# A two-layer diffusion step: the zeroing, three weight places, one modulation unit and one semaphore are moved

## The reference

```
for i in (0, 1):
    sh_a, sc_a, g_a, sh_f, sc_f, g_f = split(silu(cond) @ w_ada[i] + b_ada[i], 6)   # one set for context, one for latent
    h = layernorm(x) * (1 + sc_a) + sh_a
    out = diff_attention(h) @ w_attn_out   if i == 0   else   fourier_mix(h) @ w_fourier_out
    x = layernorm(alpha * x + g_a * out) * ln_gain[i, 0] + ln_bias[i, 0]
    h = layernorm(x) * (1 + sc_f) + sh_f
    y = sum over the top 2 of 8 experts in the top 1 of 4 groups of  w * (silu(h @ w_gate) * (h @ w_up)) @ w_down
    x = layernorm(alpha * x + g_f * y) * ln_gain[i, 1] + ln_bias[i, 1]
```

## Time and profile before

| | |
|---|---|
| median of 3 runs | 1018.64 us (1015.99 to 1021.48) |
| the profiled execution's own time | 1015.99 us |
| its span | 1014.2 us |
| its granted TensorE clock, mean | 0.933 of full speed |
| TensorE matmul busy | 852.1 us (84%) |
| VectorE, ScalarE, GpSimd busy | 342.7, 147.6, 164.8 us |
| moved by DMA | 324.69 MB, mean 320 GB/s |

### The profile page before, as it was taken

The page is one execution under the profiler, slowest core; times in us unless marked ns, Lnnn a source line. Parts: engine busy times, 40 slices in busy tenths (PEclk is TensorE's granted clock), DMA queues, the critical chain, the costliest instruction groups (busy, mean ns, idle before and its releaser), DMA issues.

```text
span 1014.2 us, 12948 instructions
## 1 busy us (share of the span) xinstructions
PE 852.1 (84%) x4983; PEld 441.9 (44%) x4983; DVE 342.7 (34%) x836; ACT 147.6 (15%) x341; POOL 164.8 (16%) x250
## 2 busy tenths in 40 slices
PE   3899999998997889988788787999599878787864
PEld 2556565655475333333233335766433333332321
DVE  3113455565784111111111159347511111111147
ACT  1122222224011010110000113111111000100010
POOL 1041111122112020211111001211111111111100
PEclk9999999999987999999899999999589989998988
DMA  9996584267368996999999779863889999999941
GB/s 336 366 370 242 182 327 177 84 251 261 125 238 348 375 415 267 418 418 419 418 420 418 321 299 388 306 248 137 328 350 419 419 419 418 418 421 417 392 170 62
DMA packets 91181, 324.69 MB, mean 320 GB/s; under 512 B 12590, under 2 KB 25614, under 8 KB 66520
## 3 DMA queue, kind: packets, MB, share of 16 engines
q1 hardware_dynamic: 73360, 287.97, 72.0%
q0 software_dynamic: 12704, 21.86, 6.0%
q10 hardware_dynamic: 5032, 13.71, 3.4%
HBM read 313.75 MB, written 32.05 MB: 341 GB/s over the span
## 4 chain that ended last, share of the span: by engine, by line
PE 54%; DMA 29%; DVE 10%; issue 3%; ACT 2%; POOL 1%; SPq 1%; ACTq 0%; POOLq 0%; DVEq 0%
PE psum L993 17%; DMA ring<-in_w_expert_up 16%; PE psum L876 8%; PE psum L823 6%; PE psum L1015 5%; DMA h_hT<-in_w_expert_up 4%; PE psum L772 4%; PE psum L848 3%; DMA ring<-in_w_ada 3%; PE psum L980 2%; DMA arena<-h_scratch,gidx 2%; DMA y_scratch<-arena,sidx 1%; PE psum L1204 1%; PE psum L1078 1%; PE psum L927 1%
## 5 line engine op out<-in xcount | busy, mean ns | idle before, releaser
L993 PE MATMUL psum<-ring,arena 128*64 128x512 f32 x880 | 267.2, 648 | 39.0 <-DMA ring<-in_w_expert_up 25.6
L993 PEld LDWEIGHTS psum<-ring,arena 128*64 128x64 f32 x880 | 88.1, 149 | 175.5 <-issue 172.0
L1015 PE MATMUL psum<-ring,arena 128*64 128x512 f32 x440 | 125.8, 603 | 20.1 <-DVE arena L1781 19.4
L1777 DVE TENSOR_TENSOR arena<-arena,psum 128x256 f32<-128x256 f32 x34 | 14.3, 421 | 296.8 <-ACT arena L1328 296.8
L993 PE MATMUL psum<-h_hT,arena 128*64 128x512 f32 x208 | 101.9, 647 | 10.2 <-DMA ring<-in_w_expert_up 9.3
L876 PE MATMUL psum<-ring,h_hT 128*128 128x384 f32 x288 | 98.0, 494 | 0.0
L823 PE MATMUL psum<-ring,h_hT 128*128 128x512 f32 x160 | 69.5, 593 | 1.1 <-ACT h_hT L1412 0.7
L876 PEld LDWEIGHTS psum<-ring,h_hT 128*128 128x128 f32 x288 | 54.4, 194 | 34.9 <-issue 1.6
L636 POOL DMA_INDIRECT y_scratch<-arena,sidx x32 | 32.7, 1021 | 227.0 <-DVE arena L1787 227.0
L1015 PEld LDWEIGHTS psum<-ring,arena 128*64 128x64 f32 x440 | 36.0, 137 | 71.3 <-issue 46.9
L772 PE MATMUL psum<-ring,silu 128*32 128x128 f32 x1536 | 52.7, 299 | 14.5 <-DMA ring<-in_w_ada 14.5
(11 more groups left out here) (207 smaller groups left out, 914.1 us busy)
## 6 DMA issues: line engine op xcount, KB each, us to landing
ring<-in_w_expert_gate SPq DMA_DIRECT2D x52, 1024.0 KB, 17.2
ring<-in_w_expert_up SPq DMA_DIRECT2D x52, 1024.0 KB, 23.9
ring<-in_w_expert_down SPq DMA_DIRECT2D x52, 1024.0 KB, 25.8
ring<-in_w_ada SPq DMA_DIRECT2D x24, 2048.0 KB, 15.1
h_hT<-in_w_expert_gate SPq DMA_DIRECT2D x12, 1024.0 KB, 18.2
h_hT<-in_w_expert_up SPq DMA_DIRECT2D x12, 1024.0 KB, 22.8
h_hT<-in_w_expert_down SPq DMA_DIRECT2D x12, 1024.0 KB, 25.6
ring<-in_w_qkv SPq DMA_DIRECT2D x9, 1024.0 KB, 12.4
```

The source lines that it names most:

```text
L993: last = pe.matmul(bank[b][64 * e:64 * e + 64, :].rearrange("p (g n) -> p g n", g=2), mem.GT[b][:, c, 64 * e:64 * e + 64], w, start=(c == ...
L1015: last = pe.matmul(bank[5 + half][64 * e:64 * e + 64, :], mem.actT[b][:, f, 64 * e:64 * e + 64], w[:, f, 512 * half:512 * half + 512], sta ...
```

## The change

1. **Zeroing.** The two transfers that zero `y_scratch` (3 MB each, from SBUF to DRAM) stood in the attention, one behind each of the last two quarters of `w_qkv`. Both now stand behind expert 0 of layer 0, ahead of unit (1, 1).
2. **Places.** Units (1, 3), (1, 4), (1, 5) go from C1, A0, A1 to A0, A1, A2. C1 is so free after unit (1, 1), and expert 1 of layer 0 is loaded then, not after unit (1, 3). Unit (1, 3) is now loaded when `w_attn_out` has been used, with (1, 4), and unit (1, 5) when (1, 2) has been computed.
3. **Unit (1, 9)** is computed ahead of the Fourier product of the context, not ahead of (1, 8); its add on VectorE moves ahead of the evictions of the turned tiles. Its transfer stays where it was.
4. **Semaphores.** `lam_in` is dropped: all seven transfers count on `ctx_in`, and both VectorE (before the lambda products) and TensorE (before the attention) wait for 16 * 7. The transpose of the condition counts on a new `cond_ps`, and the waits on `col_ps` are one lower.

```diff
-PLACE.update({("ada", 1, u): place for u, place in enumerate(("A2", "C1", "A2", "C1", "A0", "A1"))})
+PLACE.update({("ada", 1, u): place for u, place in enumerate(("A2", "C1", "A2", "A0", "A1", "A2"))})
...
             for u in (2, 3):
                 sp.wait_ge(qkv_ps, 6 * u - 6)
                 load_qkv(u, slice(0, 8), place_in[f"Q{u % 2}"])
-                sp.wait_ge(zeroed, 5)
-                sp.dma_start(y_dram[u - 2].rearrange("(c p) n -> p c n", p=P), bc(mem.zero.unsqueeze(1), [P, 2 * TILES, D])
-                             ).then_inc(scratch_out, 16)
...
             load("ada", 1, 0)
             sp.wait_ge(qkv_ps, 18)
             load_expert(0, 0)
+            sp.wait_ge(zeroed, 5)
+            for l in range(2):
+                sp.dma_start(y_dram[l].rearrange("(c p) n -> p c n", p=P), bc(mem.zero.unsqueeze(1), [P, 2 * TILES, D])
+                             ).then_inc(scratch_out, 16)
             sp.wait_ge(qkv_ps, 24)
             load("ada", 1, 1)
-            for u in (2, 3):
-                after_ada(1, u - 2)
+            after_ada(1, 0)
+            load("ada", 1, 2)
+            after_ada(1, 1)
+            load_expert(0, 1)
+            sp.wait_ge(proj_ps, 6)
+            for u in (3, 4):
                 load("ada", 1, u)
-            sp.wait_ge(proj_ps, 6)
-            for u in (4, 5):
-                load("ada", 1, u)
-            after_ada(1, 3)
-            load_expert(0, 1)
+            after_ada(1, 2)
+            load("ada", 1, 5)
             after_ada(1, 5)
...
-            pe.wait_ge(ctx_in, 32)
+            pe.wait_ge(ctx_in, 16 * 7)
...
             over_channels(0)
             pe.wait_ge(sums_read, 2)
+            ada(1, 9)
             pe.wait_ge(chan_act, 4)
...
-            for u in (9, 8, 10, 11):
+            for u in (8, 10, 11):
                 ada(1, u)
...
-                act.dma_start(mem.lam[:, n, :], A[name][0].partition_broadcast(P)).then_inc(lam_in, 16)
-            act.dma_start(mem.gain8[:, :], A["subln_gain"][0].partition_broadcast(P)).then_inc(lam_in, 16)
+                act.dma_start(mem.lam[:, n, :], A[name][0].partition_broadcast(P)).then_inc(ctx_in, 16)
+            act.dma_start(mem.gain8[:, :], A["subln_gain"][0].partition_broadcast(P)).then_inc(ctx_in, 16)
             act.dma_start(mem.ctxk, A["cache_k"][0, 0].rearrange("s h d -> s (h d)")).then_inc(ctx_in, 16)
             act.dma_start(mem.ctxv, A["cache_v"][0, 0].rearrange("s h d -> s (h d)")).then_inc(ctx_in, 16)
...
-            dve.wait_ge(lam_in, 16 * 5)
+            dve.wait_ge(ctx_in, 16 * 7)
...
             layer_end()
+            ada_add(1, 9)
             dve.wait_ge(col_done, 3)
             turn_evict(1, 1)
             turn_evict(1, 2)
-            for u in (9, 8, 10, 11):
+            for u in (8, 10, 11):
                 ada_add(1, u)
```

More of the change, by code:

```diff
@@ L282, in build @@
         h_dram = [nc.dram_tensor(f"h_scratch{l}", (2 * TOK, D), F32).ap() for l in range(2)]
-        first_in, router_in, x_in, lam_in, ctx_in = (sem(n) for n in ("first_in", "router_in", "x_in", "lam_in", "ctx_in"))
+        first_in, router_in, x_in, ctx_in = (sem(n) for n in ("first_in", "router_in", "x_in", "ctx_in"))
         spread_in, root_out = sem("spread_in"), sem("root_out")
@@ L291, in build @@
         down_landed = [sem(f"down_landed{i}") for i in range(SLOTS)]
-        silu_done = sem("silu_done")
+        cond_ps, silu_done = sem("cond_ps"), sem("silu_done")
         ada_ps, ada_done = sem("ada_ps"), sem("ada_done")
@@ L828, in _ @@
             pe.wait_ge(first_in, 48)
-            pe.transpose(bank[0][:, 0:2 * KC], mem.cond[:, :], mem.const("ident")[0:2 * KC, 0:2 * KC]).then_inc(col_ps, 1)
+            pe.transpose(bank[0][:, 0:2 * KC], mem.cond[:, :], mem.const("ident")[0:2 * KC, 0:2 * KC]).then_inc(cond_ps, 1)
             pe.wait_ge(silu_done, 2)
@@ L1245, in _ @@
                               ).then_inc(bias_in, 16)
-            act.wait_ge(col_ps, 1)
+            act.wait_ge(cond_ps, 1)
             for i in range(2):
@@ L1487, in columns_in @@
             def columns_in(part):
-                dve.wait_ge(col_ps, part + 2)
+                dve.wait_ge(col_ps, part + 1)
                 V.tensor_copy(mem.col[:, :, part, :, :],
@@ L1493, in columns @@
             def columns(l):
-                dve.wait_ge(col_ps, l + 3)
+                dve.wait_ge(col_ps, l + 2)
                 V.tensor_copy(mem.col[:, :, :, :, :].rearrange("p s u j i -> p (s u j) i"),
```

## The result

| | median | ratio to the kernel before | 95% interval |
|---|---|---|---|
| the changed kernel, first measurement | 1044.41 us (1040.97 to 1045.45, 4 runs; before 1018.88, 4 runs) | 1.0246 | 1.0209 to 1.0283 |
| the changed kernel, second measurement (`again_all`, other runs of before beside it) | 1047.89 us (6 runs; before 1018.62, 10 runs) | 1.0286 | 1.0251 to 1.0322 |

The changed kernel is 2.5 to 2.9% slower than the kernel before. The forecast was 1046 us. The profiled execution of the first measurement took 1042.27 us, its span is 1040.5 us (before 1014.2), its mean granted clock 0.929.

What follows compares the result with a forecast made beforehand. TensorE was taken to bound the kernel, save where DMA streams the experts' weights. The terms 3.7 + 10.0 + 5.4 + 9.3 = 28.4 us on 1016.0 gave 1044.4, by the median 1047.0; forecast 1046 us, range 1030 to 1056.

Steps and rivals of the forecast that it cites:

- The chain (VectorE, ACT, `rope`, TensorE): Before the attention: VectorE waits 4.15 us longer for `cache_v`, delaying ACT, `rope` and TensorE; less POOL's spare 0.5, 3.7 us.
- TensorE restarts slowly: After a new stall TensorE runs at a lower clock, costing 1.2 to about 4 us more; 2 taken.
- the gap behind: Behind unit (1, 1): TensorE's gap at 250.18 takes up 1.1 us of the 9.1 us lateness, leaving 8.0.
- POOL's way: Part 1's second way: POOL's root for head 6, behind the zeroings, comes 5.3 us late, covered by the 8.0.
- by about 242 the zeroings have landed: Behind expert 0 of layer 0: both zeroings, taking 15.1 us, land by about 242, when POOL issues its row transfers.
- the first rival: At units (1, 1) and (1, 4): some waits absent or made up for; 1036 or about 1028 us; chance 0.19.
- what comes back: Part 2, around the first gather: 3.7 us of TensorE's wait and 1 us of slow clock return against 10.1 lost.
- The gather's wait: First gather of layer 0: with expert 1 out of its way, TensorE no longer waits until 323.36, giving back 3.7 us.
- Some of the slow clock may go as well; I take -1: Behind the first gather: part of the slow clock after TensorE's wait goes, giving back 1 us.
- The expert stage, read as moving along with its first pairs: Layer 0's experts: whatever delays TensorE's first pair delays the whole stage as much; its length stays as before.
- the rival for a faster kernel: First gather: expert 1's early load decides, part 2 giving 5 and up to 9 us back; 1013 us, faster 0.04.
- POOL was blocked: Rival at the zeroings: they land only at 250 us, delaying root, columns and unit 8 us more; 1055 us, chance 0.06.

Runs made afterwards that it cites:

- p1_unit_first: The kernel before with only the zeroings moved, placed behind unit (1, 1) and ahead of unit (1, 2): 1031.48 us, ratio 1.0164.
- after: The changed kernel with all four parts against the kernel before, first measurement and its profiled execution: 1044.41 us, ratio 1.0246.
- p2_alone: The kernel before with the places of part 2 alone changed: 1020.68 us, ratio 1.0038.
- best: The kernel before with expert 1's down matrix loaded behind unit (1, 1) and unit (1, 9) computed between turn_tile(1) and turn_tile(2): 1010.27 us, ratio 0.9947.

## Why the prediction was right

The time was right (1046; 1044.4 and 1047.9 measured), and so was its sign at every part. The sum was better than its terms (in brackets the price by stage without what is told under the table of stages):

| part | forecast, bounds | measured by stage | by ratio, alone |
|---|---|---|---|
| 4, semaphore | 3.7 (3.0 to 4.2) | 6.0 (6.9) | 7.5 |
| 1, zeroing | 10.0 (5.3 to 14) | 10.2 (10.6) | 15.0 |
| 2, places | 5.4 (1 to 9) | 3.1 | 3.9 |
| 3, unit (1, 9) | 9.3 (7.3 to 11) | 7.9 | 9.2 |
| sum | 28.4 | 27.2 (28.5) | 35.6 |

- **Part 4 was mis-sized, and outside its bounds.** The chain (VectorE, ACT, `rope`, TensorE) held, and the 3.7 us for its wait were 4.0, counted from the issue of `cache_v`. (In the changed kernel's profile L894 is 5.6 us later, but 1.4 us of that is a later issue of `cache_v`, 51.25 and not 49.85, from a unit (0, 2) that took 3.42 us and not 1.96, as in several kernels without the part.) What the term left out is the step "TensorE restarts slowly", which I had charged to parts 1 and 3 only: 2.9 us more.
- **Part 1's steps held on TensorE's way.** 9.1 us late was forecast; from unit (0, 4) to unit (1, 1) all kernels with the part take 9.0 to 9.4 us more. (The sum itself was slightly off: 248.7 and half of 2.5 us are 249.95 and not 249.7, so 9.3 us late.) 2 us were put for the clock and 1.1 taken off for the gap behind, 0.9 in all; from the unit to the offsets the five kernels take 1.4 us more (0.8 to 1.8). In the changed kernel it is 1.7 us: 1.7 for the unit at half clock (3.64 us), 0.5 us for `project_head` behind it, less only 0.5 us from the gap, which is still 0.58 us long. The Trainium skill's 358 GB/s (DMA: Bandwidth & Descriptors, Specifications) gave an estimate of 12.5 us for the part; the rows' 418 came nearer. **POOL's way was mis-sized**: "by about 242 the zeroings have landed". Unit (1, 1)'s own 2.1 MB take 5.0 us at 418 GB/s, so its bytes began at 228.6 in the kernel before, and by the same sum the zeroings should have been put 15.1 us behind that, at 243.7; they landed at 251.83 - 7.5 = 244.3 in the old count. (Its sum had a slip too: 242 + 3.3 are 245.3, 5.0 us late and not 5.3.) Its 5.3 us were 7.4. It changes nothing here, for it is covered, but as the lower bound and as the first rival's price it was too small, and `p1_unit_first` shows that there was no easy half of this part to be lost.
- **Part 2: the wait was right, what comes back was mis-sized.** 10.1 us late was forecast for the unit; it starts 8.6 us later against the offsets in `after` and 9.7 in `p2_alone`, takes some 1 us more itself at half clock, and the positions come 9.6 and 10.5 us later. The gather's wait gave 2.7 and 3.9 of it back (forecast 3.7). "Some of the slow clock may go as well; I take -1": nearly all of it went, 3.8 and 3.7 us between the first gather's transposes and pair 1.
- **Part 3 was right in each step.** The unit landed 20.6 us after its issue, L1185 follows it, VectorE's 2 us fell away. The 2 us for the clock were too many: the unit at half clock took 3.52 us, 1.6 more, and L1185 behind it (3.84 us, 3.81 in the earlier trace rows) lost nothing. The remaining 1 us between 9.3 and 7.9 is in part the reference: the kernels without the part took 52.1 us on average, the profiled execution of the kernel before 51.5.
- **The sum.** Part 4's cost was put 2.3 to 3.2 us too low, part 2's 2.3 and part 3's 1.4 us too high; that these cancel is luck and not skill. The first two errors come from the slow clock, which was put at nothing in part 4 and at 1 us given back in part 2. The expert stage, read as moving along with its first pairs, did: 253.7 us before, 252.4 and 253.5 after. That `cond_ps` costs nothing was argued and not tried by itself.
- **The rivals.** None of the three waits was missing, and none was much shorter than forecast: 8.98, 6.63 and 10.13 us in the changed kernel, with 6.63 the lowest of six at unit (1, 4) (to 10.74). The gather did profit from expert 1's early load, as the rival for a faster kernel said, by some 7 us (10 us late, 3.1 left). It didn't decide, because unit (1, 4) landed nearly when forecast: TensorE started on it 26.8 us (`after`) and 27.8 us (`p2_alone`) behind the offsets, forecast 28.4. `best` is that rival without the stall. POOL was blocked 2 us longer than forecast and not 8.

## What to carry to other kernels

A transfer that is moved ahead of others on a queue delays all that stand behind it, and a computation that is moved ahead of others gains nothing if its transfer stays: for each, compare the landing of its bytes with the time at which the engine comes to it. A stall of TensorE that wasn't there cost here its length and 1.4 to 2.9 us of half clock behind it, and a stall taken away ahead of heavy matmuls gave 3.7 us of that back; this belongs in each term, not in one. A second waiter on the same landing (POOL here) has to be timed by the same sum, because it can take over when the first one is cured.

## What the runs showed of the hardware

- How long TensorE's work ran at half clock was not in proportion to its stall: 3.4 us behind an idle time of 0.77 us (before, from 69 us on), 8.3 us behind 4.89 us of waiting for `rope` (after), but only one unit of 3.52 us behind 10.13 us of waiting for unit (1, 9). In the changed kernel the clock was at half for 10.2 us in each of three places (from 70.7, 251.6 and 640.7 on). It fell while TensorE stood idle each time, and what differs is how much of the 10.2 us TensorE still spent waiting: 2, 5.5 and 7 us.
- A unit of 64 matmuls takes 1.95 us at full clock and 3.4 to 3.6 us at half, and in the same place of the same code it may be either: unit (0, 2) took 1.96 us in the kernel before and 3.42 us in the changed one, behind waits of 1.76 and 1.80 us. A cost of the clock read from one execution can be off by that much. Where the clock is the same, the distances of marks repeat closely (204.1 to 204.4 us to the offsets in six kernels), while the 95% intervals of the ratios above reach 2.4 to 5.8 us to each side.
